# Dilated attention's entry reordered, and the stick attention's scores split over both halves of the array's rows

## The chip, the cores and the metric

One core of a Trainium2 chip runs the whole program. The engines work beside each other and meet through semaphores: TensorE (PE; its weight loads are the rows PEld) multiplies into the eight banks of PSUM, VectorE (DVE), ScalarE (ACT) and GpSimd (POOL) do the elementwise work, and SyncE (SP) issues the weight loads. The metric is device microseconds of one execution, the median of the runs. TensorE's clock is granted at one of two levels, 1.2 or 2.4 GHz; the profile gives the granted share.

## What is computed

Two blocks of two layers each on 512 tokens of width 1024: a state-space mixer and a stick-breaking attention with their gated MLPs, then an even mixer (a chunked gated MLP beside a dilated attention) and a gated linear attention with convolutional MLPs. The change touches the stick attention and the entry of the even mixer's dilated attention:

```python
# stick-breaking attention, 16 heads of 64; per block of 128 queries
z = jnp.einsum('bhqd,bhkd->bhqk', qb, kb) * scale
log_beta = jax.nn.log_sigmoid(z)
log_1m_beta = jnp.where(past, jax.nn.log_sigmoid(-z), 0.0)
between = lax.cumsum(log_1m_beta, axis=3, reverse=True) - log_1m_beta
weights = jnp.where(past, jnp.exp(log_beta + between), 0.0)
outs.append(jnp.einsum('bhqk,bhkd->bhqd', weights.astype(vb.dtype), vb))

# even mixer: gated MLP beside 8 heads of dilated attention
a_out = chunked_gmlp(gelu(u), gelu(v), a_ln_g, a_ln_b, a_ws, a_bs)
qh, kh, vh = rms_norm(heads(q), q_g), rms_norm(heads(k), k_g), heads(vb)
# three branches of softmax(qk / 8) v with windows and strides, mixed by their log-sums
out = jnp.concatenate([a_out, b_out], axis=-1).astype(h.dtype) @ w_out
```

## The kernel before

Each engine has its own program, written out stage by stage, and waits by hand on counting semaphores; nothing is scheduled by a tool. Weights come as tiles of 1 MB, two buffers in turn. Each is split into a rounded high part (ScalarE, L1562) and the rest (VectorE, L2207), and a product of two such numbers is three matmuls (hi x hi, hi x lo, lo x hi). Plain 32-bit operands take two passes over the array for one matmul, so the trace shows twice as many matmuls as the program has.

**Stick attention** (`stick_attention`, L1104 to L1170). Q and K lie with the features on partitions, two heads of 64 features one above the other: an even head on rows 0 to 63, an odd one on rows 64 to 127. `stick_scores(h)` writes the scores of head h, keys on partitions, into the three banks 4 (h mod 2) to 4 (h mod 2) + 2: a mask matmul (L1109), then the four blocks of a key block with its own queries (L1114, first bank), then the later queries of key blocks 0, 2 and 1 (L1120, 384, 128 and 256 columns; second and third bank). All have 64 rows, those of the head. The loop runs scores of head h+1, the running sums of head h (`stick_sums`, L1130 to L1142), then half a mix of an earlier pair of heads (`stick_mix`, L1153 or L1161) from h = 2 on. VectorE and ScalarE work on each head's scores in two parts, own blocks and later queries: absolute value (L2389), exponential (L1680), logarithm (L1686), combination (L2398), and after the sums the weights' exponential (L1693). `z_done` counts the scores' two releases, `w_done` the two halves of weights, after which the banks are free. Before, the mask waits for the first half of head h-2's weights and the later queries for the second. GpSimd is idle in this stretch.

**Entry of dilated attention.** After the q and k features of the even mixer (stage ev_qk) TensorE does the gated MLP's products (L1210, `gm_bank` 5, 6, 7, 3) and eight mean squares of the heads' q and k (L1220, banks 0 to 3 in turn). VectorE adds the bias (L2569) and multiplies into `u_feat` (L2573, `gm_copied`); then it builds the table of score biases (L2575 to L2588). ScalarE squares the features (L1778), takes the logarithms of the mean squares (L1780, `qk_ln`) and one exponential over all (L1783, `qk_rstd`); VectorE then scales q and k of two pairs of heads (`stage_pair`, L2618). TensorE waits for all eight logarithms, computes the values (stage ev_vb, `token_stage`: eight units of 24 matmuls on 128 tokens and 256 columns, banks 0 to 7, L1088 to L1090), and only then the scores of heads 0 and 1 (L1234). VectorE adds the biases and takes the row maxima (`rows`, L2599, L2603), ScalarE exponentiates (L1790) and normalises (L1797) by VectorE's reciprocal (L2608). Then runs the steady loop of eight heads: transposing the probabilities ("turn", L1244), a copy of them by ScalarE (L1802), scores two heads ahead (L1234), and the product with the values (`mix`, L1255). The weights' splitting for the next stage lies among it: VectorE's second one (L2207) stands between the rows of head 1 and the reciprocal of head 0.

The linear attention of the second block is not touched, but one of its loops is read below: its state products alternate between the two halves of the array's rows, and each half writes its own banks:

```python
for a in range(2):
    for hf in range(2):
        rows = slice(hf * 64, hf * 64 + 64)
        n = 4 * m + 2 * a + hf
        if n < GLA_CHUNKS - 1:
            mm = nc.tensor.matmul(bank[2 * hf + m][:, a * GLA_DV:(a + 1) * GLA_DV], gks_t[rows, n // 2, h, :],
                                  gvt[rows, n // 2, h * GLA_DV:(h + 1) * GLA_DV], start=True, stop=True)
```

## Time and profile before

| | |
|---|---|
| median of 3 runs | 2556.47 us (2555.90 to 2556.67) |
| the profiled execution | 2554.76 us, its span 2553.0 us |
| mean granted clock of TensorE | 0.981 |
| busy share of the span | PE 96%, PEld 79%, DVE 48%, ACT 32%, POOL 12% |
| chain that ended last | PE 89%, DVE 7%, ACT 2%, POOL 1% |

Times in the rows are microseconds from the span's start. A row of the timeline merges equal instructions that follow each other: the first number is the start, the second the length, and x14 says how many. Behind the row stands, in brackets, how long its engine was idle and what ended that.
### The profile page before, as it was taken

The page shows a single profiled execution, that of the slowest core. Times are in us where ns is not written, and L with a number is a line of the kernel's source. Part 1 is how long each engine was busy: PE and PEld are TensorE (multiplying, and loading weights), DVE is VectorE, ACT ScalarE, POOL GpSimd, SP SyncE. Part 2 cuts the span into 40 slices and gives each one's busy share as a digit, 9 for nine tenths or more (in the row PEclk, how much of TensorE's full clock was granted, in tenths as well). Part 3 has the DMA queues.
Part 4 walks back from the last instruction along what each step waited for, and adds up shares of the span by engine and source line. Part 5 has one row for each costly group of instructions (what it writes and reads, how often), then busy time and mean ns, then how long its engine had stood idle before and what let it go on. Part 6 is the DMA issues. An engine that isn't in the chain of part 4 may idle for free.

```text
span 2553.0 us, 32215 instructions
## 1 busy us (share of the span) xinstructions
PE 2459.4 (96%) x12941; PEld 2017.4 (79%) x12941; DVE 1233.3 (48%) x1618; ACT 824.9 (32%) x923; POOL 304.7 (12%) x213
## 2 busy tenths in 40 slices
PE   7699999999999989999989989999999999999999
PEld 6587788887897668888858758888889986988887
DVE  8835433345435564333544464555434445644432
ACT  5422322223225523222243363333323243432222
POOL 6503000004000040000221013000023001100000
PEclk8899999999999989999999989999999999999999
DMA  2432232233320013322342211323233221233232
GB/s 54 92 103 92 83 98 91 77 102 95 99 86 14 11 56 99 99 93 80 91 121 67 67 34 50 108 92 98 85 93 105 83 83 50 83 99 99 84 91 90
DMA packets 254438, 210.30 MB, mean 82 GB/s; under 512 B 7156, under 2 KB 252298, under 8 KB 254250
## 3 DMA queue, kind: packets, MB, share of 16 engines
q1 hardware_dynamic: 250682, 205.99, 26.2%
q8 instruction: 102, 1.67, 0.3%
q0 software_dynamic: 976, 1.74, 0.3%
q10 hardware_dynamic: 2656, 0.72, 0.1%
q14 instruction: 22, 0.18, 0.0%
HBM read 203.97 MB, written 2.10 MB: 81 GB/s over the span
## 4 chain that ended last, share of the span: by engine, by line
PE 89%; DVE 7%; ACT 2%; POOL 1%; issue 1%; DMA 0%; SPq 0%; DVEq 0%; POOLq 0%; ACTq 0%
PE psum L845 14%; PE psum L847 14%; PE psum L846 14%; PE psum L975 9%; PE psum L976 9%; PE psum L977 9%; PE psum L1088 2%; PE psum L1089 2%; PE psum L1090 2%; POOL tmp_a L575 1%; PE psum L1120 1%; PE psum L1138 1%; PE psum L926 1%; PE psum L927 1%; PE psum L928 1%
## 5 line engine op out<-in xcount | busy, mean ns | idle before, releaser
L1562 ACT CAST w_hi<-w_stage 128x2048 fp32r<-128x2048 f32 x209 | 400.4, 1916 | 1341.2 <-PE psum L847 714.5
L2207 DVE TENSOR_TENSOR w_lo<-w_stage,w_hi 128x2048 fp32r<-128x2048 f32 x202 | 473.8, 2345 | 634.5 <-ACT w_hi L1562 634.4
L975 PE MATMUL psum<-x_hi,w_hi 128*128 128x512 f32 x864 | 341.1, 395 | 19.9 <-DVE x_lo L2343 16.1
L845 PE MATMUL psum<-x_hi,w_hi 128*128 128x512 f32 x888 | 345.9, 390 | 0.0
L846 PE MATMUL psum<-x_lo,w_hi 128*128 128x512 f32 x888 | 345.5, 389 | 0.0
L847 PE MATMUL psum<-x_hi,w_lo 128*128 128x512 f32 x888 | 345.5, 389 | 0.0
L976 PE MATMUL psum<-x_lo,w_hi 128*128 128x512 f32 x864 | 339.7, 393 | 0.0
L977 PE MATMUL psum<-x_hi,w_lo 128*128 128x512 f32 x864 | 339.3, 393 | 0.0
L845 PE MATMUL psum<-hidden_hi,w_hi 128*128 128x512 f32 x746 | 291.4, 391 | 0.8 <-DVE w_lo L2207 0.8
L847 PE MATMUL psum<-hidden_hi,w_lo 128*128 128x512 f32 x746 | 290.3, 389 | 0.0
L846 PE MATMUL psum<-hidden_lo,w_hi 128*128 128x512 f32 x746 | 290.2, 389 | 0.0
L975 PEld LDWEIGHTS psum<-x_hi,w_hi 128*128 128x128 f32 x864 | 164.4, 190 | 58.4 <-issue 23.5
L845 PEld LDWEIGHTS psum<-x_hi,w_hi 128*128 128x128 f32 x888 | 166.7, 188 | 35.2 <-issue 0.7
L847 PEld LDWEIGHTS psum<-x_hi,w_lo 128*128 128x128 f32 x888 | 166.7, 188 | 34.7
L846 PEld LDWEIGHTS psum<-x_lo,w_hi 128*128 128x128 f32 x888 | 166.7, 188 | 34.4
L977 PEld LDWEIGHTS psum<-x_hi,w_lo 128*128 128x128 f32 x864 | 164.3, 190 | 34.7
L976 PEld LDWEIGHTS psum<-x_lo,w_hi 128*128 128x128 f32 x864 | 164.5, 190 | 34.0
L845 PEld LDWEIGHTS psum<-hidden_hi,w_hi 128*128 128x128 f32 x746 | 140.0, 188 | 30.8 <-issue 2.1
L846 PEld LDWEIGHTS psum<-hidden_lo,w_hi 128*128 128x128 f32 x746 | 140.0, 188 | 29.5 <-issue 0.5
L847 PEld LDWEIGHTS psum<-hidden_hi,w_lo 128*128 128x128 f32 x746 | 140.0, 188 | 29.2
L565 POOL TENSOR_TENSOR tmp_a<-residual 128x512 f32<-128x512 f32 x4 | 7.2, 1793 | 945.3 <-DVE residual L2252 831.0
L1088 PE MATMUL psum<-w_hi,x_hi 128*128 128x256 f32 x384 | 109.6, 285 | 0.8 <-ACT qk_rstd L1780 0.8
(436 smaller groups left out, 3437.9 us busy)
## 6 DMA issues: line engine op xcount, KB each, us to landing
w_stage<-in_ffn_w_gu_dram SPq DMA_DIRECT2D x44, 1024.0 KB, 5.1
w_stage<-in_ffn_w_down_dram SPq DMA_DIRECT2D x64, 704.0 KB, 4.6
w_stage<-in_ffn_w_gate_dram SPq DMA_DIRECT2D x22, 1024.0 KB, 5.2
w_stage<-in_ffn_w_up_dram SPq DMA_DIRECT2D x22, 1024.0 KB, 5.4
w_stage<-in_sb_w_qkv_dram SPq DMA_DIRECT2D x12, 1024.0 KB, 5.1
w_stage<-in_od_w_in_dram SPq DMA_DIRECT2D x12, 1024.0 KB, 5.3
w_stage<-in_ev_w_in_dram SPq DMA_DIRECT2D x10, 1024.0 KB, 5.1
w_stage<-in_ssm_w_glu_dram SPq DMA_DIRECT2D x8, 1024.0 KB, 5.5
```

Source lines behind the costliest of these rows:

```text
L575: sum_link(nc.gpsimd.tensor_tensor(acc_sq, acc_sq, dev_slot[c], ALU.add))
L845: nc.tensor.matmul(dst, hi, x_hi, start=(start and k == 0), stop=False)
L846: nc.tensor.matmul(dst, hi, x_lo, start=False, stop=False)
L847: mm = nc.tensor.matmul(dst, lo, x_hi, start=False, stop=(stop and k == kn - 1))
L975: nc.tensor.matmul(dst[u], hi, x_hi, start=(k == order[0]), stop=False)
L976: nc.tensor.matmul(dst[u], hi, x_lo, start=False, stop=False)
L977: mm = nc.tensor.matmul(dst[u], lo, x_hi, start=False, stop=(k == order[-1]))
L1088: nc.tensor.matmul(dst, hi, wh[:, k, :], start=(k == 0), stop=False)
L1089: nc.tensor.matmul(dst, hi, wl[:, k, :], start=False, stop=False)
L1090: mm = nc.tensor.matmul(dst, lo, wh[:, k, :], start=False, stop=(k == DC - 1))
L1562: nc.scalar.copy(whi[:, half, :], wst[:, half, :]).then_inc(whi_done, 1)
L2207: V.tensor_tensor(wlo[:, half, :], wst[:, half, :], whi[:, half, :].bitcast(F32), ALU.subtract).then_inc(wlo_done, 1)
```

## The change

**Scores on both halves of the rows.** Two new tiles of 2 KB a partition, `q_swapped` and `k_swapped`, hold one head's q and k on the half of the partitions that is not its own. GpSimd fills them by two DMAs a head (64 partitions of 2 KB, SBUF to SBUF): heads 0 and 1 once the k stage is done, head h from the end of head h-2's scores, each pair after the pair before has landed (`swap_landed`). `stick_scores` now waits, before the first own block, for both halves of head h-2's weights and for the copies. Then it runs own block 0, the later queries of key block 0 on the other half, own blocks 1 and 2, the later queries of key block 2 on the other half, own block 3 (first release) and the later queries of key block 1 on the own half (second release).

**Entry of dilated attention.** The mean squares go to banks 0, 1, 2 and 4, and chunk 3 waits for the first product of the gate instead of the fourth. The values' banks are 5, 6, 7, 3 for the first half of the columns and 4, 0, 1, 2 for the second; the first half waits for the gate's banks one by one, only the second half for all logarithms. The scores of heads 0 and 1 stand behind the first and second unit of the second half and use the first half's banks. VectorE's rows, reciprocals and value copies are woven into that order, both of its splits of the next stage's weights come later, and ScalarE normalises head 0 before it exponentiates head 1; ScalarE's two casts of the weight tiles stand before head 0 and after head 1.

```diff
-                half = slice((h % 2) * 64, (h % 2) * 64 + 64)
+                own, other = slice(h % 2 * 64, h % 2 * 64 + 64), slice(64 - h % 2 * 64, 128 - h % 2 * 64)
...
                 if h >= 2:
                     pe.wait_ge(w_done, 2 * (h - 2) + 2)
...
+                pe.wait_ge(swap_landed, 32 * (h + 1))
+                own_block(0)
+                later_queries(0, other, k_swap, q_swap)
+                own_block(1)
+                own_block(2)
+                later_queries(2, other, k_swap, q_swap)
+                own_block(3).then_inc(z_done, 1)
+                later_queries(1, own, k_f[:, h // 2, :], q_f[:, h // 2, :]).then_inc(z_done, 1)
```

```diff
+            pool.wait_ge(evac_done, ST["k"].evac1)
+            for h in range(HEADS):
+                own, other = slice(h % 2 * 64, h % 2 * 64 + 64), slice(64 - h % 2 * 64, 128 - h % 2 * 64)
+                if h >= 2:
+                    pool.wait_ge(z_done, 2 * (h - 2) + 2)
+                if h >= 1:
+                    pool.wait_ge(swap_landed, 32 * h)
+                pool.dma_start(q_swap[other, :], q_f[own, h // 2, :]).then_inc(swap_landed, 16)
+                pool.dma_start(k_swap[other, :], k_f[own, h // 2, :]).then_inc(swap_landed, 16)
```

```diff
                     if c == 3:
 
-                        pe.wait_ge(gm_copied, 4)
+                        pe.wait_ge(gm_copied, 1)
...
+                pe.wait_ge(wlo_done, st.it0 * 2 + 1)
+                for n in range(TT):
+                    pe.wait_ge(gm_copied, n + 1)
+                    value_unit(0, n)
+                pe.wait_ge(wlo_done, st.it0 * 2 + 2)
+                pe.wait_ge(qk_ln, 8)
+                for n in range(TT):
+                    value_unit(1, n)
+                    if n < 2:
+                        early_scores(n)
```

How the order changes, at the places that are spoken of below. On TensorE, one steady round of the stick attention before, from the mask to the first sum:

```order
L1109 MATMUL psum<-not_past,ident_rounded 128x512 [waits w_done]
L1114 MATMUL psum<-q_feat,k_feat 128x128 x4
L1120 MATMUL psum<-q_feat,k_feat 128x384 [waits w_done]
L1120 MATMUL psum<-q_feat,k_feat 128x128
L1120 MATMUL psum<-q_feat,k_feat 128x256
```

The same round now (q_swapped and k_swapped are the other half of the rows):

```order
L1125 MATMUL psum<-not_past,ident_rounded 128x512 [waits w_done]
L1131 MATMUL psum<-q_feat,k_feat 128x128 [waits swap_landed,w_done]
L1135 MATMUL psum<-q_swapped,k_swapped 128x384
L1131 MATMUL psum<-q_feat,k_feat 128x128 x2
L1135 MATMUL psum<-q_swapped,k_swapped 128x128
L1131 MATMUL psum<-q_feat,k_feat 128x128
L1135 MATMUL psum<-q_feat,k_feat 128x256
```

The second wait for the weights moved from the later queries to the first own block, and the two matmuls of the other half stand among the own blocks.

On VectorE, from the last scaled pair of heads to the first reciprocal, before (prob is a head's rows, value_tok the values):

```order
L2618 SCALAR_TENSOR_TENSOR kn_pair<-qk_feat,params,qk_rstd 128x512
L2219 UNCONDITIONAL_BRANCH
L2378 COPY value_tok<-psum 128x256 [waits part_done] x4
L2207 TENSOR_TENSOR w_lo<-w_stage,w_hi 128x2048 [waits whi_done]
L2378 COPY value_tok<-psum 128x256 [waits part_done] x4
...
L2603 TENSOR_REDUCE even_stats<-prob 128x1 [waits sm_done]
L2207 TENSOR_TENSOR w_lo<-w_stage,w_hi 128x2048 [waits whi_done]
L2608 RECIPROCAL even_stats<-even_stats 128x4 [waits pexp]
```

The same place now; the rows left out at the two dots are those of heads 0 and 1:

```order
L2649 COPY value_tok<-psum 128x256 [waits part_done] x4
...
L2649 COPY value_tok<-psum 128x256 [waits part_done]
L2665 RECIPROCAL even_stats<-even_stats 128x4 [waits pexp]
...
L2649 COPY value_tok<-psum 128x256 [waits part_done]
L2261 TENSOR_TENSOR w_lo<-w_stage,w_hi 128x2048 [waits whi_done]
L2649 COPY value_tok<-psum 128x256 [waits part_done] x2
L2261 TENSOR_TENSOR w_lo<-w_stage,w_hi 128x2048 [waits whi_done]
L2705 UNCONDITIONAL_BRANCH
L2665 RECIPROCAL even_stats<-even_stats 128x4 [waits pexp]
```

The first reciprocal moved ahead of both splits, and the second one, of head 1, stands behind both.

## Rows read from the trace of the kernel before

**Rows 1.** Stage table, stick attention: stretch, length, busy time by engine (count), clock, DMA, GB/s

```profile
788.80:886.20 97.40, 97.40 (x573) 64.55 (x572) 58.00 (x101) 55.85 (x79) 0.00 (x0) 1.00 0.00 1
```

**Rows 2.** Timeline, one head's scores, and the weights that free the next banks

```profile
801.89 1.16 PE L1114 MATMUL psum<-q_feat,k_feat 64*128 64x128 f32 x8
...
802.88 1.46 PE L1120 MATMUL psum<-q_feat,k_feat 64*128 64x384 f32 x6
...
804.28 1.12 PE L1130 MATMUL psum<-stick,neg_up_to 128*128 128x512 f32 x2
...
808.05 0.81 ACT L1693 ACTIVATE stick<-psum 128x768 f32<-128x768 f32 x1 [0.52 <-PE psum L1142]
...
809.41 1.16 PE L1114 MATMUL psum<-q_feat,k_feat 64*128 64x128 f32 x8
```

**Rows 3.** Timeline of TensorE, state products of the linear attention, two heads

```profile
2084.99 0.49 PE L1350 MATMUL psum<-gla_v_tok,gla_k_tok 64*128 64x256 f32 x2
...
2092.62 1.99 PE L1350 MATMUL psum<-gla_v_tok,gla_k_tok 64*128 64x256 f32 x14
```

**Rows 4.** Timeline, the same round, VectorE's first and ScalarE's last step on the scores

```profile
803.08 0.69 DVE L2389 TENSOR_SCALAR stick<-psum 128x512 int32<-128x512 int32 x1
...
806.60 0.93 ACT L1686 ACTIVATE stick<-stick,one_col 128x768 f32<-128x768 f32 x1
```

**Rows 5.** Timeline, a round without a mix

```profile
780.02 0.81 ACT L1693 ACTIVATE stick<-psum 128x768 f32<-128x768 f32 x1 [0.52 <-PE psum L1142]
...
780.15 1.16 PE L1114 MATMUL psum<-q_feat,k_feat 64*128 64x128 f32 x8
...
786.43 1.16 PE L1114 MATMUL psum<-q_feat,k_feat 64*128 64x128 f32 x8
```

**Rows 6.** Line L603: two 128 KB loads on GpSimd's queue, issue ns and landing us

```profile
L603 POOL DMA_DIRECT2D d_rows<-in_ev_a_bs_dram x2: 627/640/654, 1324.8 to 1325.5; - x2
...
DMA to landing us min/median/max: 4.4/4.4/4.4
```

**Rows 7.** Timeline of TensorE at the entry of dilated attention

```profile
1443.37 1.19 PE L1220 MATMUL psum<-even_squares,head_mean 128*128 128x512 f32 x1 [3.77 <-DVE u_feat L2573]
...
1451.62 0.38 PE L1088 MATMUL psum<-w_hi,x_hi 128*128 128x256 f32 x1 [0.78 <-ACT qk_rstd L1780]
...
1486.39 2.57 PE L1244 MATMUL psum<-ident,prob 128*128 128x128 f32 x10 [6.09 <-ACT prob L1797]
...
1497.54 1.31 PE L1244 MATMUL psum<-ident,prob 128*128 128x128 f32 x10
...
1503.43 0.77 PE L1244 MATMUL psum<-ident,prob 128*128 128x128 f32 x5
```

**Rows 8.** Timelines of VectorE and ScalarE at the entry of dilated attention

```profile
1438.55 0.69 DVE L2573 TENSOR_TENSOR u_feat<-u_feat,mixed 128x512 f32<-128x512 f32 x1
...
1440.63 0.69 ACT L1780 ACTIVATE qk_rstd<-psum,eps_rms 128x512 f32<-128x512 f32 x1
...
1475.00 1.91 ACT L1562 CAST w_hi<-w_stage 128x2048 fp32r<-128x2048 f32 x1 [9.61 <-PE psum L1090]
...
1476.08 0.29 DVE L2599 SCALAR_TENSOR_TENSOR prob<-psum,score_bias 128x128 f32<-128x128 f32 x1 [0.70 <-PE psum L1234]
...
1479.16 0.69 DVE L2603 TENSOR_REDUCE even_stats<-prob 128x1 f32<-128x512 f32 x1
...
1483.44 2.28 DVE L2207 TENSOR_TENSOR w_lo<-w_stage,w_hi 128x2048 fp32r<-128x2048 f32 x1
...
1485.84 1.93 ACT L1797 ACTIVATE prob<-prob,even_stats 128x128 f32<-128x128 f32 x4 [1.47 <-DVE even_stats L2608]
```

**Rows 9.** Stage table, entry of dilated attention: the same columns as rows 1

```profile
1443.40:1450.80 7.40, 7.40 (x10) 2.84 (x10) 4.06 (x11) 3.27 (x5) 0.00 (x0) 0.60 0.01 2
1451.60:1474.90 23.30, 23.28 (x192) 23.08 (x192) 7.73 (x12) 5.54 (x2) 0.00 (x0) 1.00 0.14 46
...
1486.40:1497.50 11.10, 11.10 (x26) 5.49 (x26) 4.09 (x9) 6.83 (x16) 0.00 (x0) 0.52 0.29 94
```

More of the change, by code:

```diff
@@ L2370, in copy_stage, with token_stage @@
                 stage_loop(name, body)
[L2372 removed]
+            def token_stage(name, dst):
                 st = ST[name]
@@ L2379, in body @@
                                           bank[4 * half + n][:, 0:256]).then_inc(evac_done, 1)
-                        if not (hold and half):
-                            split_next(half)
+                        split_next(half)
                 stage_loop(name, body)
@@ L2636, in dilated_attention @@
                 stage_pair(0, 1)
-                values()
-                rows(0, 0)
-                rows(1, 1)
-                split(ST["ev_vb"].it0 + 1, 1)
+                for n in range(TT):
+                    value(0, n)
+                rows(0, 0, first_scores)
+                value(1, 0)
                 sums(0, 0)
+                rows(1, 1, first_scores)
+                value(1, 1)
+                split(st.it0 + 1, 0)
+                value(1, 2)
+                value(1, 3)
+                split(st.it0 + 1, 1)
                 with dve.Fori(0, HEADS_B // 4 - 1) as i:
```

84 lines of the change are left out of this document (53 added, 31 removed).

## The prediction

> **What bounds the kernel now.** I read the page's chain first, then the two stretches that the diff touches. The chain is nearly all TensorE: work taken from TensorE, or a stall taken from it, moves the end. The stick attention is such work: from 788.8 to 886.2 TensorE is busy all the time at the full clock while VectorE and ScalarE are busy 58.0 and 55.9 of 97.4 us [rows 1]. The entry of dilated attention is the other kind. There TensorE stands idle 3.77 us for `u_feat`, then runs at a fallen clock, then waits 6.09 us for the first head's `prob`, and again runs at half clock [rows 7, 9]. A reader should see in both that what ends late is named in the row: TensorE itself in the first, ScalarE and VectorE in the second.
>
> **Stick scores.** One head's scores are eight passes for the own blocks from 801.89 to 802.88 (0.99 us) and six for the later queries until 804.28, where the sums start; 0.09 of that is the turn to a full-height load, so 1.30 [rows 2]. Those six passes stream 1536 columns, 0.85 ns a column: 0.11 us for 128 columns, 0.22 for 256, 0.32 for 384, with 0.11 for the first weight load. All use one half of the array's rows. The change puts the later queries of key blocks 0 and 2 (two passes of 0.32, two of 0.11) on the other half. If the halves run beside each other, the own half is the longer one: 0.11 + 8 x 0.11 + 2 x 0.22 = 1.43 us instead of 2.29 (0.86 with rounding). Do they? The state products of the second block's linear attention alternate between the halves at 64 rows and 256 columns: the first two passes, 0.48 us each, lie within 0.49 us; and fourteen passes take 1.99 us, where in a row they would take 0.11 + 14 x 0.22 and a tail of 0.16, 3.35 us, and where the half with eight passes alone gives 0.11 + 8 x 0.22 + 0.16 = 2.03 [rows 3]. So the longer half sets the time, and I take 0.86 for each of 16 heads, 13.8 us; with no overlap it is nothing, which stays as the other bound.
>
> The Trainium skill ("TensorE: Matmul & The Clock Gate", Packing small matmuls) says that matmuls start and end strictly in program order, one FIFO for all tiles. By that rule the third to sixth own passes wait behind the long pass of the other half and a head's scores take about 1.65 us. The rows speak against it: in program order the second pass of the lower half stands ahead of the first of the upper half, yet the first passes of both lie in 0.49 us.
>
> What it adds: the own blocks now also wait for the second half of the weights of head h-2 (w_done, from L1693). At the steady pace ScalarE ends that one at 808.86 and the own blocks start at 809.41 [rows 2]: 0.55 us to spare. Queued behind the waiting matmul are all of TensorE's sums. Cover is gone where there is no mix yet: there L1693 runs from 780.02 to 780.83 and the own blocks started at 780.15 [rows 5]. The scores' first release comes no earlier than before (own block 3 ends with the eighth pass of its half in both), so the loop through VectorE and ScalarE must be walked too: own blocks to L2389 1.19, on to the second L1686 3.52, that one 0.93, L1693 0.81, and about 0.1 to TensorE: 6.55 us a head [rows 2, 4]. TensorE's period there is 809.41 less 801.89 = 7.52, after the change 6.66: still the longer, by 0.1. In the rounds without a mix it is 6.28 [rows 5], would be 5.4, and the loop wins: counted in old times, head 2's own blocks start at 780.3 (L1693 is ready 0.6 earlier, since the sums are), head 3's 6.55 later at 786.9 instead of 786.43, and its scores end at 788.3 instead of 788.7. Heads 1 to 3 together gain 0.4 instead of 2.6. So 0.86 (head 0, among value matmuls) + 0.4 + 12 x 0.86 = **11.6 us**.
>
> The copies: 32 of 128 KB on GpSimd's queue, none in the trace. The nearest row is a 128 KB load on that queue, 0.64 us to issue and 4.4 to land [rows 6]; two in flight, about 5.5 us. The copy for head h goes out when the scores of h-2 are done and is wanted nearly two periods (some 12 us) later; GpSimd has nothing else there until the next norm, and the DMA engines move 1 GB/s [rows 1]. I take them at zero; what they cost if late is a rival.
>
> **Entry of dilated attention.** Step one: the mean square of chunk 3 waits for the first of L2573 (ends 1439.24) instead of the fourth; it started at 1443.37, and the next ten passes ran at a mean clock of 0.60 [rows 7 to 9]. Freed, its two passes of 512 columns (0.43 each) end at about 1440.4, and the rest is paced by ScalarE: busy with the logarithm of chunk 2 until 1441.32, then one square and five logarithms of up to 0.69, started a little closer [rows 8], to about 1444.8. The last mean square is out by 1443.8; the values take other banks and start at about 1443.9 instead of 1451.62: 7.7 us.
>
> Step two: the 192 value passes stay 23.1 us [rows 9], and two heads' scores go between them, 2.4 us each (twice 1280 columns at 0.85 ns, and 0.2 for the load and the turn). Rows, exponentials and normalising of head 0 run beside the value units of 2.9 us. So the values end at 1443.9 + 23.1 + 4.8 = 1471.8, with the turns back to the values' form 1472.2, and turn 0 follows at 1472.3 instead of 1486.39: 14.1 us.
>
> Step three: turn 0 to turn 1 took 11.15 us, of which nearly all at a clock of 0.52; at the full clock a round takes 1497.54 to 1503.43, 5.9 [rows 7, 9]. With no idle stretch ahead I expect the full clock, 6.05 with the waits: 5.1 more, **19.2 us** at turn 1. Head 1's `prob` is the narrow point: ScalarE casts the second weight tile (1.91) only after 1472.3, VectorE splits it (2.28) until 1476.6, then ScalarE normalises (1.93) until 1478.8 [rows 8]. Turn 1's last transposes wait for that.
>
> Step four, given back: head 2's rows (3.8 us, as head 0's from 1476.08 to 1479.85) [rows 8] start only at 1476.8, so its exponentials end about 1481.6, ahead of which ScalarE may not copy turn 1: 1.0 us; and stage_pair ends behind head 3's rows, 0.8 us late for head 4's scores. After that TensorE is the longest again. 19.2 - 1.8 = **17.4 us**. Bounds: 19.2 if VectorE keeps up, 9.3 if the clock falls as before (below).
>
> Sum: 17.4 + 11.6 = 29.0. The profiled execution took 2554.8 us (span 2553.0); it would take 2525.8. The median of the runs is 1.7 above it, so 2556.5 - 29.0 = **2527.5 us**.
>
> **Rivals.**
> - Starts in order. A pass of the upper half does not overtake waiting passes of the lower. Then, from the first load, own 0 starts at 0.11 and 0.22, the long passes at 0.22 and 0.54, own 1 and 2 from 0.54 to 0.88, the other half's short ones at 0.88 and 0.99, own 3 at 0.99 and 1.10, the last two at 1.21 and 1.43, and the end is 1.65 instead of 1.43: 0.2 less saved on 13 heads, 2.8 us: 2530. For it: one pair of passes and one total are thin evidence. Against: [rows 3]. The skill's FIFO rule, above, is this case.
> - No overlap at all: the scores cost 2.29 as before. 2539. Against: [rows 3]; for: there each product wrote its own bank from fresh, here they add to a bank with a mask.
> - The loop through VectorE and ScalarE binds. 6.55 against 6.66 is close, and every second head VectorE evacuates a mix ahead of L2389. If every round costs half a microsecond more, the attention gains 5: 2534.
> - The clock falls again at the entry, since ScalarE paces the mean squares and head 1's `prob` is late. Then the two cold stretches stay, 3.0 us of the first (7.4 x 0.4) and 5.1 of the second: 2535.6.
> - **Slower than before:** the copies. Head h's go out only when those of h-1 have landed, so a round can't be shorter than one pair's issue and landing. If two 128 KB copies don't overlap, 2 x (0.64 + 4.4) = 10.1 us a round [rows 6] against 7.7 before (the 97.4 us of [rows 1] hold twelve such rounds and a short one of 4.7): 14 x 2.4 = 33 us. With the scores' gain gone and the entry's 17.4 left the kernel takes 2572. From a pair time of 7.7 + 17.4 / 14 = 8.9 us it is slower than before; below 6.6 the copies cost nothing. Against: loads on this queue were in flight together when their 4.4 was taken.
>
> **How the numbers follow.** Forecast 0.66 (its own range 2522 to 2533), starts in order 0.10, no overlap 0.05, the loop 0.09, the clock 0.07, slower 0.03. The fastest end is the full 13.8 and 19.2, 2523.5, less 2 us for clock changes elsewhere, since all later idle stretches shift: 2521. The upper end, 2537, takes in all rivals but no overlap and the copies. A measurement of this kernel tells 0.2% (5 us) from no change. Only the copies reach that bound or cross it: faster 0.96, same 0.01, slower 0.03.
>
> **What would show it.** In the stick attention: 1.5 us from the first own pass to the sums, 0.86 us less between the sums of successive heads, no wait of TensorE longer than 0.2 us except in the first two rounds, copies landing in 3 to 6 us. At the entry: the value matmuls start 7 to 8 us earlier after the gate's, there is no idle over 1.5 us, the clock is 1.0 throughout, and turn 1 comes 34 us after the first value matmul instead of 45.9. Wrong if the passes of the two halves follow each other, if TensorE waits for `swap_landed`, if the gap before turn 1 is over 2 us, or if the stage after the entry gives the time back waiting for weights.

## The result, and the profile after

The changed kernel takes 2524.45 us (median of 4 runs, 2523.96 to 2528.27) against 2556.18 (2553.92 to 2556.67) for the kernel before beside it. The ratio is 0.9881, 95% interval 0.9864 to 0.9898. The profiled execution took 2524.61 us, 30.15 less than the profiled one of before. The forecast was 2527.5.

The page of the changed kernel, its span and the granted clock in 40 slices:

```profile
span 2522.9 us, 32268 instructions
...
PEclk9899899999999999999999999999999999999999
```

To see where 30.1 us went, I took four marks from the timelines of both kernels: the first mask of the stick attention, the end of its last running sums (L1138, now L1162), the gate's first matmul (L1210, now L1234), the end of the last mix of dilated attention. The offset is the time after less the time before.

| mark | before | after | offset | gained since the mark above |
|---|---|---|---|---|
| first mask | 762.08 | 765.18 | +3.10 | -3.1 |
| last sums end | 889.32 | 879.95 | -9.37 | **12.46** |
| gate's first matmul | 1432.28 | 1420.51 | -11.77 | 2.4 |
| last mix ends | 1537.17 | 1507.03 | -30.14 | **18.37** |
| end of the span | 2553.0 | 2522.9 | -30.1 | 0 |

The two bold stretches are what the diff touches. The other two entries belong to code that is the same in both kernels. There the granted clock differs: from 240 to 260 us it is 1.00 before and 0.83 after; from 946 to 962 it is 0.74 before, and in the same work of after, 938 to 950, 0.86; from 1332 to 1348 it is 0.89 before, and in the same work of after, 1323 to 1339, 1.00. They nearly cancel.

The two changed stretches, busy times of each engine, then the granted clock. First before:

```profile
762.08:889.32 127.24, 127.24 (x752) 87.70 (x751) 75.11 (x130) 70.29 (x96) 0.00 (x0) 1.00 0.03 9
...
1432.28:1537.17 104.89, 90.53 (x482) 60.08 (x481) 61.15 (x121) 63.19 (x125) 10.22 (x12) 0.90 0.09 31
```

and after:

```profile
765.18:879.95 114.77, 113.43 (x752) 78.12 (x751) 73.91 (x130) 67.54 (x96) 14.41 (x28) 1.00 0.17 42
...
1420.51:1507.03 86.52, 82.39 (x482) 57.31 (x481) 60.51 (x120) 62.26 (x125) 10.19 (x12) 1.00 0.11 37
```

In the first, TensorE's instructions are the same in number (752) and its busy time fell by 13.8 us; 1.34 us of idle time is new. In the second, the clock rose from 0.90 to 1.00 and TensorE's idle time fell from 14.4 to 4.1 us.

**One head's scores** in the changed kernel, TensorE's timeline (the counterpart of [rows 2]; L1131 are the own blocks, L1135 the later queries, L1154 the sums):

```profile
795.05 0.37 PE L1131 MATMUL psum<-q_feat,k_feat 64*128 64x128 f32 x1
...
795.06 0.59 PE L1135 MATMUL psum<-q_swapped,k_swapped 64*128 64x384 f32 x1
...
795.26 0.38 PE L1131 MATMUL psum<-q_feat,k_feat 64*128 64x128 f32 x2
...
795.48 0.48 PE L1135 MATMUL psum<-q_swapped,k_swapped 64*128 64x384 f32 x1
...
795.49 0.49 PE L1131 MATMUL psum<-q_feat,k_feat 64*128 64x128 f32 x3
795.80 0.27 PE L1135 MATMUL psum<-q_swapped,k_swapped 64*128 64x128 f32 x1
...
796.04 0.59 PE L1135 MATMUL psum<-q_feat,k_feat 64*128 64x256 f32 x2
...
796.57 1.12 PE L1154 MATMUL psum<-stick,neg_up_to 128*128 128x512 f32 x2
```

Both halves start within 0.01 us. From the first own pass to the sums it is 1.52 us, where before it was 2.39. In the program the second long pass of the swapped tiles stands ahead of the second own block; in the trace it waits for its half until 795.48, while the own pass behind it began at about 795.37 (the second of the two at 795.26, 0.11 apart). So a waiting pass of one half doesn't stop the other half. The Trainium skill ("TensorE: Matmul & The Clock Gate", Packing small matmuls) says that matmuls keep program order in start and in end; this timeline disagrees on the start, and the measurement decides. (The ends of matmuls are modelled in the trace, so it says less of them.)

**The entry**, TensorE's timeline from the mean squares to the scores of head 4 (the counterpart of [rows 7]; L1244 mean squares, L1269 the early scores, L1302 turns, L1313 mixes, L1292 later scores):

```profile
1424.98 7.16 PE L1244 MATMUL psum<-even_squares,head_mean 128*128 128x512 f32 x16
...
1446.45 2.42 PE L1269 MATMUL psum<-kn_pair,qn_pair 64*128 64x128 f32 x8
...
1460.09 1.25 PE L1302 MATMUL psum<-ident,prob 128*128 128x128 f32 x10
...
1465.92 1.39 PE L1302 MATMUL psum<-ident,prob 128*128 128x128 f32 x10
...
1470.32 2.37 PE L1313 MATMUL psum<-prob_t,vb_pair 128*64 128x512 f32 x8 [0.65 <-ACT prob_t L1854]
1472.61 1.31 PE L1302 MATMUL psum<-ident,prob 128*128 128x128 f32 x10
1474.67 2.39 PE L1292 MATMUL psum<-kn_pair,qn_pair 64*128 64x128 f32 x8 [0.74 <-issue]
```

All sixteen mean squares run in one piece and the values follow at 1431.58. Turn 0 starts 39.57 us after the gate's first matmul (before: 54.11), turn 1 at 45.41 (before: 65.25). The last two rows with brackets are the only new waits.

### The profile page after: what moved, and what is told of

It is laid out like the page before. It is cut to its first block, busy times and chain, and to the rows that moved or that the text cites. A ratio compares the mean times of both kernels' runs of the same rounds, so it can differ in the third digit from the quotient of the medians.

```text
span 2522.9 us, 32268 instructions
## 1 busy us (share of the span) xinstructions
PE 2439.9 (97%) x12941; PEld 2005.0 (79%) x12941; DVE 1231.4 (49%) x1617; ACT 820.6 (33%) x923; POOL 321.0 (13%) x245
## 4 chain that ended last, share of the span: by engine, by line
PE 90%; DVE 4%; ACT 2%; POOL 2%; issue 1%; SPq 1%; DMA 0%; POOLq 0%; DVEq 0%; ACTq 0%
PE psum L861 15%; PE psum L862 15%; PE psum L863 15%; PE psum L991 9%; PE psum L992 9%; PE psum L993 9%; PE psum L1104 2%; PE psum L1105 2%; PE psum L1106 2%; POOL tmp_a L581 1%; SPq L451 1%; PE psum L942 1%; PE psum L1162 1%; PE psum L943 1%; PE psum L944 1%
## 5 line engine op out<-in xcount | busy, mean ns | idle before, releaser
L2261 DVE TENSOR_TENSOR w_lo<-w_stage,w_hi 128x2048 fp32r<-128x2048 f32 x202 | 473.8, 2345 | 631.2 <-ACT w_hi L1614 631.2
L861 PEld LDWEIGHTS psum<-hidden_hi,w_hi 128*128 128x128 f32 x746 | 140.0, 188 | 31.1 <-issue 2.1
L2292 DVE TENSOR_TENSOR tmp_b<-psum,tmp_a 128x512 f32<-128x512 f32 x52 | 36.0, 692 | 120.8 <-PE psum L863 120.8
```

Source lines behind the costliest of these rows:

```text
L861: nc.tensor.matmul(dst, hi, x_hi, start=(start and k == 0), stop=False)
L2261: V.tensor_tensor(wlo[:, half, :], wst[:, half, :], whi[:, half, :].bitcast(F32), ALU.subtract).then_inc(wlo_done, 1)
L2292: V.tensor_tensor(tmp_b[:, u, :], bank[2 + u][:, :], tmp_a[:, u, :], ALU.mult).then_inc(evac_done, 1)
```

## The experiments

The runs were taken in three groups, each beside its own runs of the kernel before, whose medians were 2555.6 (e1 to e4), 2556.58 (e5 to e8) and 2555.03 us (e9 to e12). The medians scatter by 2 us or so with the clock elsewhere, so beside each median stands the length of the two stretches of the table, which repeat to 0.02 us.

| run | median us | ratio, 95% interval | stick attention | dilated attention |
|---|---|---|---|---|
| before | 2556.18 | | 127.24 | 104.89 |
| changed | 2524.45 | 0.9881 (0.9864 to 0.9898) | 114.78 | 86.52 |
| e1_scores_only | 2540.58 | 0.994 (0.9924 to 0.9957) | 114.78 | 103.11 |
| e2_entry_only | 2539.18 | 0.9935 (0.9919 to 0.9952) | 127.24 | 86.52 |
| e3_copies_own_half | 2536.86 | 0.9923 (0.9906 to 0.9939) | 130.39 | 86.53 |
| e4_bunched | 2524.85 | 0.988 (0.9864 to 0.9897) | 116.34 | 86.53 |
| e5_split_late | 2528.82 | 0.9889 (0.9866 to 0.9912) | 114.78 | 87.44 |
| e6_mean_square_wait | 2531.15 | 0.9905 (0.9888 to 0.9924) | 114.78 | 93.11 |
| e7_scores_behind_values | 2531.72 | 0.9906 (0.9888 to 0.9923) | 114.78 | 95.57 |
| e8_own_first_heads_2_3 | 2525.43 | 0.9882 (0.9864 to 0.9901) | 113.87 | 86.53 |
| e9_changed_again | 2523.21 | 0.9881 (0.9865 to 0.9898) | 114.78 | 86.53 |
| e10_improved | 2520.14 | 0.9869 (0.9852 to 0.9885) | 113.85 | 85.09 |
| e11_copies_late | 2523.96 (one run) | | 114.78 | 86.53 |
| e12_other_half_last | 2527.78 (one run) | | 119.88 | 86.53 |

### The two parts alone

e1 is the kernel before with the swapped tiles, their copies and the new score order; e2 is the changed kernel with the old scores.

> The kernel before with the stick attention's part of the change alone: the two swapped tiles, their 32 copies on GpSimd, and the seven score calls in the new order over both halves of the rows. The entry of dilated attention is the old one (its semaphore `tables` is folded into sm_done, at the same place). My theory, that the two parts add and that the whole trace difference of 30.1 us is 12.5 in the stick attention (from the first mask to the last sums 124.2 against 111.7 us), 18.4 at the entry, and the rest clock changes of 3 us of either sign elsewhere: 2556.2 - 12.5 = 2543.7, within 3 us; sums 6.65 and 7.06 us apart, as in the changed kernel. The prediction's own term was 11.6: 2544.6. Rival 1, the attention's gain comes only together with the new entry (its part is given back before the entry, at a wait for weights): 2553 or more. Rival 2, most of the 30 us is the attention and the entry alone brings under 12: 2538 or less.

> The changed kernel with the old stick scores: no swapped tiles, no copies, fourteen passes on one half of the rows. The entry of dilated attention is the new one. My theory: 18.4 us less than before, 2537.8, within 3 us; the prediction's term was 17.4, 2538.8. Turn 1 comes 45.4 us after the gate's first matmul as in the changed kernel, and TensorE's clock is 1.0 there. Rival, the clock's good behaviour at the entry is luck of the phase, and depends on when the stage begins: with the stage 12 us later one cold stretch of 6.8 us returns, 3.4 us lost, 2541.2 or more.

Measured: 15.0 and 16.4 us less than before, 31.4 together, against 31.1 for the changed kernel by the same runs of before. In the stretches the parts add exactly: 12.46 in the stick attention with or without the new entry, 18.37 at the new entry with or without the new scores. The old entry in e1:

```profile
1417.50:1520.60 103.10, 88.74 (x482) 59.38 (x481) 61.12 (x120) 63.03 (x125) 10.22 (x12) 0.92 0.10 31
```

It takes 103.1 us instead of 104.9, with the clock at 0.92 instead of 0.90: the old entry's cost depends on how its idle stretches fall on the clock. The new entry in e2, which begins 11.8 us later than in the changed kernel, keeps the full clock:

```profile
1432.30:1518.80 86.50, 82.37 (x482) 57.28 (x481) 60.51 (x120) 62.24 (x125) 10.18 (x12) 1.00 0.11 37
```

All eight profiles that have the new entry without further changes keep 1.00 through it, with the gate's first matmul at 1416.7 to 1434.4 us. So the rival that its good clock was luck of the phase is not borne out; how near it is, e6 shows below.

### Is it the two halves, or something that came with them?

```diff
-                own_block(0)
-                later_queries(0, other, k_swap, q_swap)
-                own_block(1)
-                own_block(2)
-                later_queries(2, other, k_swap, q_swap)
-                own_block(3).then_inc(z_done, 1)
+                own_block(0)
+                own_block(1)
+                own_block(2)
+                own_block(3).then_inc(z_done, 1)
+                later_queries(0, own, k_f[:, h // 2, :], q_f[:, h // 2, :])
+                later_queries(2, own, k_f[:, h // 2, :], q_f[:, h // 2, :])
```

> The changed kernel, copies and waits kept, but the later queries of key blocks 0 and 2 read the original tiles on the own half of the rows, and all own blocks come first, as before. Nothing overlaps, so the difference to the changed kernel is the worth of the two halves, and the difference to the run with the new entry alone is what the copies and the two waits ahead of the own blocks cost. My theory: copies 0; the earlier wait for the second half of the weights makes the rounds of heads 2 and 3 take the loop's 6.55 us instead of 6.28, 0.5 us in all: 0.5 us above the entry alone, so about 2538.3 and 13.8 (0.86 times 16) above the changed kernel. Rival, the copies cost (TensorE waits for swap_landed, or their traffic slows the weights' loads): 3 us or more above the entry alone.

The stick attention took 130.39 us, 3.15 more than before and 15.6 more than the changed kernel. TensorE never waits for the copies. Of the 3.15 us, the rounds of heads 2 and 3 account for 1.48: sums 7.03 us apart instead of 6.29. The other 1.7 go with a fall of the clock between 788 and 796 us (0.79 over 8 us). It shows in the sums 2.4 us behind the second of two waits of 0.67 us. The changed kernel has the same two waits, the same copies and no such fall, so the cause stays open. The rival on the copies had named 3 us or more, which is the size; but no wait for a copy is in the trace. The median lies below e2's in spite of it; with the clock elsewhere differing, the medians can't tell 3 us here.

My price for the earlier wait was wrong: 0.74 us a round, not 0.27. The timeline of e3 in the round of head 2, ScalarE and TensorE:

```profile
779.85 0.81 ACT L1745 ACTIVATE stick<-psum 128x768 f32<-128x768 f32 x1 [0.52 <-PE psum L1166]
...
780.72 1.16 PE L1131 MATMUL psum<-q_feat,k_feat 64*128 64x128 f32 x8 [0.67 <-ACT stick L1745]
```

The second exponential of the weights, L1745, is released by TensorE's own last sums (L1166), not by the logarithm. The loop that binds is scores (2.38), sums until that exponential may start (3.77), the exponential (0.81) and the step back to TensorE (0.06): 7.02. In the changed kernel it is the same chain with 1.52 for the scores, 6.16:

```profile
777.60 1.12 PE L1154 MATMUL psum<-stick,neg_up_to 128*128 128x512 f32 x2
...
781.38 0.81 ACT L1745 ACTIVATE stick<-psum 128x768 f32<-128x768 f32 x1
...
782.24 0.37 PE L1131 MATMUL psum<-q_feat,k_feat 64*128 64x128 f32 x1 [0.67 <-ACT stick L1745]
```

### The loop of the first rounds

If it is that chain, own blocks that don't wait for L1745 shorten it. They write only the first bank, which the first half of the weights frees.

```diff
+                if h in (2, 3):
+                    own_block(0)
+                    own_block(1)
+                    own_block(2)
+                    own_block(3).then_inc(z_done, 1)
                 if h >= 2:
                     pe.wait_ge(w_done, 2 * (h - 2) + 2)
                 pe.wait_ge(swap_landed, 32 * (h + 1))
+                if h in (2, 3):
+                    later_queries(0, other, k_swap, q_swap)
+                    later_queries(2, other, k_swap, q_swap)
+                    later_queries(1, own, k_f[:, h // 2, :], q_f[:, h // 2, :]).then_inc(z_done, 1)
+                    return
```

> The changed kernel, but for heads 2 and 3 (the rounds that have no mix) the four own blocks come first and only then the wait for the second half of the weights and for the copies; the later queries follow as in the bunched run. It tests what binds those rounds. In the changed kernel the sums of heads 2 and 3 come 6.16 us after the previous ones: 1.52 of scores, 3.78 of sums until ScalarE may start its second exponential of weights (0.81), and the own blocks wait for that. My theory: it is this chain, so with the own blocks ahead of the wait the rounds take 5.6 us each, 1.1 us less in all, 2523.4. The prediction's theory, the way through |z|, exponential and logarithm on VectorE and ScalarE binds at 6.1 to 6.5: the rounds stay at 6.1 or more, 2524.5.

The rounds take 5.70 and 5.72 us, 0.91 less together. The timeline of e8, where L1755 is the exponential of the weights and L1164 the sums:

```profile
779.56 0.81 ACT L1755 ACTIVATE stick<-psum 128x768 f32<-128x768 f32 x1
...
779.68 0.93 PE L1131 MATMUL psum<-q_feat,k_feat 64*128 64x128 f32 x6
780.42 0.59 PE L1135 MATMUL psum<-q_swapped,k_swapped 64*128 64x384 f32 x1
...
781.49 1.12 PE L1164 MATMUL psum<-stick,neg_up_to 128*128 128x512 f32 x2
```

The own blocks start while L1755 runs, and only the later queries wait for its end at 780.37. VectorE and ScalarE keep up at 5.7 us a round, so the prediction's 6.55 for the way through them was no bound.

### How far a pass runs ahead

Two runs move the calls of the other half towards the end of the list.

e4:

```diff
-                later_queries(0, other, k_swap, q_swap)
                 own_block(1)
                 own_block(2)
-                later_queries(2, other, k_swap, q_swap)
                 own_block(3).then_inc(z_done, 1)
+                later_queries(0, other, k_swap, q_swap)
+                later_queries(2, other, k_swap, q_swap)
                 later_queries(1, own, k_f[:, h // 2, :], q_f[:, h // 2, :]).then_inc(z_done, 1)
```

e12 puts the last of these three lines ahead of the other two, so that ten passes of the own half come first.

> The changed kernel with the same seven score calls in another order: four own blocks first (with the first release), then the later queries of key blocks 0 and 2 on the other half, then those of block 1 on the own half. It tells how far a pass can run ahead of waiting passes of the other half. In the changed kernel the two halves' calls alternate in the program. A, each half has a line of its own of any length: 1.52 us from the first own pass to the sums as in the changed kernel, and its time, 2524.5. B, passes are handed out in program order and only one or two wait at each half (my theory, since the second pass on the other half stood waiting while own passes ran on): the other half gets its first pass when the own blocks are nearly through, at about 0.8 to 1.0 us, needs 0.86 us, and the last call of the own half runs beside it; 1.9 to 2.0 us, that is 0.4 to 0.5 more on 13 heads, 2530. C, no overlap at all once bunched: 2.39 us, 0.86 more on 13 heads and more, 2536.

> The changed kernel with all calls of the own half first (four own blocks, then the later queries of key block 1: ten passes), and both calls of the other half last. It measures how far a pass can run ahead in the program's order. In the bunched run the first pass of the other half began 0.55 us after the first own pass, when five of the eight own passes ahead of it had begun. A, a fixed number of passes (about three) may wait in front of it: it begins when the last own block's second pass begins, at about 0.88 us, needs 0.86 us, and the sums start 1.8 to 1.9 us after the first own pass. B, it is handed out as soon as its weights can be loaded, whatever waits: 0.55 us again, and 1.6 us to the sums. C, long passes ahead close the window: no overlap, 2.39 us.

One head in e4:

```profile
801.90 0.82 PE L1131 MATMUL psum<-q_feat,k_feat 64*128 64x128 f32 x5
802.45 0.59 PE L1135 MATMUL psum<-q_swapped,k_swapped 64*128 64x384 f32 x1
...
802.89 0.59 PE L1135 MATMUL psum<-q_feat,k_feat 64*128 64x256 f32 x2
803.20 0.38 PE L1135 MATMUL psum<-q_swapped,k_swapped 64*128 64x128 f32 x2
803.51 1.12 PE L1154 MATMUL psum<-stick,neg_up_to 128*128 128x512 f32 x2
```

and in e12:

```profile
795.32 1.04 PE L1131 MATMUL psum<-q_feat,k_feat 64*128 64x128 f32 x7
796.10 0.59 PE L1135 MATMUL psum<-q_swapped,k_swapped 64*128 64x384 f32 x1
...
797.16 1.13 PE L1154 MATMUL psum<-stick,neg_up_to 128*128 128x512 f32 x2
```

In e4 the other half's first pass begins 0.55 us in, when the fifth of eight own passes has begun; in e12 0.78 us in, when the seventh of ten has. Both times three passes of the own half stand in front of it, waiting. So in both orders a pass overtakes three and no more; that three is the limit in general rests on these two orders alone. From the first own pass to the sums: 1.61 and 1.84 us, against 1.52 in the changed order and 2.39 in one half. My B for e4 gave 1.9 to 2.0: the reach is longer than I took it. Case A of e12 held in its number of passes and in the 1.84 us; the start came 0.10 us earlier than it said.

The order has a second consequence. In e4 the second release hangs on the last call of the list (own half, 802.89 to 803.48), but the other half's last pass, which stands ahead of it in the program, ends only at 803.58. VectorE began to read these banks at 803.70. In the changed order the other half is through first, at 796.18 against 796.63. With passes that overtake, a release on the last call says nothing of the other half by itself: look in the timeline which half ends last. Whether the release waits for both, no run here shows.

### The copies

```diff
-                if h >= 2:
-                    pool.wait_ge(z_done, 2 * (h - 2) + 2)
                 if h >= 1:
+                    pool.wait_ge(z_done, 2 * (h - 1) + 2)
                     pool.wait_ge(swap_landed, 32 * h)
```

> The changed kernel with the copies for head h sent when the scores of head h-1 are done, not those of h-2. It measures how much cover the copies need, for the rival that they hold the loop up. From the release (about 1.5 us after the first own pass) to the issue 0.4, two issues of 0.52 and 2.2 to 2.4 us to land: the second copy has landed about 4.8 us after the first own pass, against rounds of 6.16 to 7.06. My theory: the sums stay 6.16, 6.65 and 7.06 us apart and nothing waits; stick attention 114.8 us. Rival, a pair costs what the prediction's slow case took, 8.9 us and more: rounds of over 8 us.

Nothing waits; all rounds are those of the changed kernel to 0.01 us. In the changed kernel the copies of q, from issue to landing:

```profile
DMA to landing us min/median/max: 2.1/2.2/5.7
```

Those of k have a median of 2.4, at most 6.5. A pair is there some 3 us after its issue. The slow rival's turning point, 8.9 us, is far off.

### The entry, step by step

e6 restores one wait:

```diff
-                        pe.wait_ge(gm_copied, 1)
+                        pe.wait_ge(gm_copied, 4)
```

> The changed kernel with the one wait restored: the mean square of chunk 3 waits again for all four u_feat instead of the first. Banks and all else stay new. It measures step one. My theory: mean square 3 starts 11.1 us after the gate's first matmul as before, the clock falls for what follows, and the values start 16.7 to 18.0 after the gate's instead of 11.07 (the run with the new scores alone had 18.1 there, with the wait for the last logarithms on top); the loss stays to the end: 5.6 to 7, so 2530 to 2531.5, and the end of the last mix at 92.1 to 93.5. Rival, TensorE catches up, since the head loop was waiting for VectorE and ScalarE anyway: 3 us or less lost, 2527.5. Rival 2, the fallen clock persists into the value matmuls: more than 8 us lost, 2532.5 or more.

```profile
1431.59 6.23 PE L1244 MATMUL psum<-even_squares,head_mean 128*128 128x512 f32 x10 [3.77 <-DVE u_feat L2626]
...
1431.60:1437.30 5.70, 5.70 (x11) 2.44 (x11) 4.05 (x10) 2.88 (x5) 0.00 (x0) 0.70 0.01 3
```

The same 3.77 us of waiting as in the kernel before is back, and the clock of the mean squares behind it falls to 0.70. The values start 16.75 us after the gate's first matmul instead of 11.07, and the last mix ends 6.59 later. The 5.68 us at the values' start stay to the end. The other 0.9 come 39 us after the values' start, at head 1's mix:

```profile
1476.00 4.06 PE L1313 MATMUL psum<-prob_t,vb_pair 128*64 128x512 f32 x8 [0.65 <-ACT prob_t L1854]
```

```profile
1476.00:1479.50 3.50, 3.50 (x6) 1.24 (x7) 3.43 (x7) 3.50 (x11) 0.00 (x0) 0.52 0.01 3
```

The clock falls there, and eight passes take 4.06 us instead of 2.37; in exchange the wait of 0.74 us behind it is gone. In the changed kernel and seven other runs the same wait of 0.65 us left the clock at 1.00. So the one restored wait is worth 5.7 of the 18.4 us, and 6.6 if the second fall is its doing, which isn't shown. The other 2.6 us at the values' start (16.75 here, 19.34 in the kernel before) are the wait for the last logarithm, which the new banks take away, and a clock of 0.60 instead of 0.70 [rows 9].

e7 keeps step one and undoes the interleaving:

```diff
                 for n in range(TT):
                     value_unit(1, n)
-                    if n < 2:
-                        early_scores(n)
+                early_scores(0)
+                early_scores(1)
```

> The changed kernel with the two early scores behind all eight value units instead of between them. It measures the interleaving, steps two and three. Walk: values end 34.3 us after the gate's first matmul; head 0's scores, rows (3.8), exponentials and normalising follow, so turn 0 begins at about 40.0 instead of 39.57; head 1's rows end at 43, both splits of VectorE (4.6) stand ahead of its reciprocal, normalised at 50, so turn 1 ends some 3.3 later than now. My theory: 3.5 to 4.5 us slower than the changed kernel at the full clock, 2528.5, end of the last mix at 90 to 91. Rival, the clock falls in the new gaps (it did in the kernel before, with a gap of 6.1 us there): 7 or more slower, 2531.5 or more. Rival 2, the order doesn't matter, since the scores need no time of their own: within 1 us of the changed kernel.

The last mix ends 9.05 us later, the median is 7.3 above the changed kernel's: the first rival. TensorE's row of turn 0, and the window of that round:

```profile
1464.48 2.37 PE L1302 MATMUL psum<-ident,prob 128*128 128x128 f32 x10 [3.88 <-DVE prob L2656]
```

```profile
1464.40:1478.00 13.60, 12.26 (x34) 6.80 (x35) 9.72 (x16) 8.17 (x18) 3.16 (x2) 0.53 0.49 155
```

A wait of 3.88 us, and the whole round after it runs at 0.53: turn 0 to turn 1 takes 12.65 us instead of 5.84. By an estimate about 5.8 of the 9.05 us are the clock (12.26 busy at 0.53). The rest, 3.3, is idle time: turn 0 starts 3.6 us later, the round holds about 1 us of waits more, and the changed kernel's two waits behind it (1.4 us) are gone. That is the pattern of the kernel before, with 6.09 us of wait and 0.52 [rows 7, 9]. More than half of what e7 loses is the clock.

### What is given back, and a faster version

Why do the two waits at 1470.32 and 1474.67 remain? VectorE in the changed kernel (L2261 the split, L2665 the reciprocal of the sums, L2675 stage_pair):

```profile
1462.27 2.29 DVE L2261 TENSOR_TENSOR w_lo<-w_stage,w_hi 128x2048 fp32r<-128x2048 f32 x1 [1.56 <-ACT w_hi L1614]
1464.48 0.17 DVE L2665 RECIPROCAL even_stats<-even_stats 128x4 f32<-128x4 f32 x1
...
1473.83 0.74 DVE L2675 SCALAR_TENSOR_TENSOR kn_pair<-qk_feat,params,qk_rstd 128x512 f32<-128x512 f32 x1
```

and ScalarE (L1849 the normalising of head 1, L1854 the copy of turn 1):

```profile
1464.69 1.92 ACT L1849 ACTIVATE prob<-prob,even_stats 128x128 f32<-128x128 f32 x4 [1.32 <-DVE even_stats L2665]
...
1469.06 1.20 ACT L1854 COPY prob_t<-psum 128x1280 f32<-128x1280 f32 x1
```

Head 1's exponentials were done at 1457.02, yet its reciprocal stands behind a split of weights that nobody needs for 40 us. e5 moves that split:

```diff
                 def heads4(i, first, last):
                     for hd in range(4):
+                        if last and hd == 2:
+                            split(st.it0 + 1, 1)
...
                 value(1, 3)
-                split(st.it0 + 1, 1)
```

> The changed kernel with one line moved: VectorE's second split of the coming weights stands before the last two heads' work instead of ahead of the head loop. It tests the prediction's step four, that this split (2.3 us) and what queues behind it give back part of the entry's gain. My theory: the reciprocal of head 1, head 2's rows and stage_pair run earlier, and TensorE's two remaining waits of the entry, 0.65 us ahead of head 1's mix and 0.74 us ahead of head 4's scores, both vanish: from the gate's first matmul to the end of the last mix 85.1 us instead of 86.5, and 2523.1. Rival, what is given back is ScalarE's doing (its cast of 1.91 us stands ahead of the copy of turn 0): the first wait stays, 0.7 less only. Rival 2, the weights' buffer comes free some 30 us later and the next stage waits for its second load: 1 to 5 us more after the attention, 2525 or more.

Both waits vanish: turn 3 comes 57.36 us after the gate's first matmul instead of 58.78, 1.42 less, as expected. But the last mix ends at 87.44, not at 85.1. The split now stands ahead of the evacuation of the last pair but one:

```profile
1498.05 2.28 DVE L2261 TENSOR_TENSOR w_lo<-w_stage,w_hi 128x2048 fp32r<-128x2048 f32 x1
...
1500.34 0.66 DVE L2594 CAST x_hi<-psum 128x512 fp32r<-128x512 f32 x1
```

and TensorE waits 2.06 us for that evacuation, after which its clock is 0.66 for 5 us. None of my three theories had it. The median, 2528.8 with runs from 2523.95 to 2532.1, also holds a slower clock elsewhere in the program.

e10 puts the split one head later, behind that evacuation (`if last and hd == 3`), where VectorE has nothing to do for 7.8 us, and takes the order of e8 for heads 2 and 3. e9 is the changed kernel beside it.

> The changed kernel itself, as the measure for the run beside it, on the same chip. Its stick attention should take the same 114.8 us from the first mask to the last sums and its dilated attention the same 86.5 us, to 0.05 us. My theory: what differs between executions of one program here is TensorE's clock in the stretches outside the two changed ones: the profiled span minus half the sum of its half-clock stretches should be the same as in the first profile within 1.5 us. Rival: DMA arrival differs, and the two stretches themselves vary by 0.3 us or more. Time 2524 to 2529.

> The changed kernel with two improvements that the runs point to. Heads 2 and 3 of the stick attention have their own blocks ahead of the wait for the second half of the weights (0.91 us less in the stick attention, as in the run of that alone), and VectorE's second split of the coming weights stands behind the evacuation of the next to last pair, where VectorE has 7.8 us with nothing to do, instead of ahead of the head loop (1.42 us less up to turn 3, as in the run with the late split; that run lost 2.1 us in turn because its split stood ahead of that evacuation, which this one doesn't). My theory: 113.9 us from the first mask to the last sums, 85.1 us from the gate's first matmul to the end of the last mix, 2.3 us less than the changed kernel in these stretches; in the median, where the clock elsewhere makes 2 us either way, between the same and 4.5 us less. Rival, the next stage then waits for its second weight load: more than 0.5 us of wait of TensorE in the 20 us after the last mix.

```profile
761.73:875.59 113.86, 113.86 (x752) 78.86 (x751) 73.75 (x130) 67.39 (x96) 14.38 (x28) 1.00 0.17 42
1418.66:1503.75 85.09, 82.25 (x482) 57.32 (x481) 60.78 (x120) 62.08 (x125) 10.23 (x12) 1.00 0.12 38
```

2520.14 us (2518.26 to 2522.17) against 2523.21 (2522.05 to 2527.3) for the changed kernel: 3.1 less in the median, 2.4 of which are the two stretches. The ratios to before, 0.9869 and 0.9881, have intervals that overlap; that it is faster rests on the stretches, which repeat to 0.02 us. In the stick attention TensorE is now busy all the time, and no wait for the weights' load follows the last mix.

My theory on e9 held for the stretches. For the rest it said that the span less half of the half-clock time should be equal. With the half-clock time that the two traces record, 60.2 us in the first profile and 77.8 in this one, it differs by 10 us, at spans that differ by 1. But the first trace's record of the clock begins only at 37.8 us, and a window ahead of it reads as full clock:

```profile
15.00:38.00 23.00, 14.82 (x128) 14.15 (x125) 21.52 (x62) 11.79 (x24) 12.58 (x10) 1.00 0.13 24
```

In e9 the same window says 0.63, with half clock from 19.2 to 36.3 us. The first trace's own matmuls show where its clock rose:

```profile
37.06 0.63 PE L745 MATMUL psum<-ident,bl_cross 128*128 128x128 f32 x2
...
37.88 0.39 PE L745 MATMUL psum<-ident,bl_cross 128*128 128x128 f32 x2
```

With e9's 17.1 us put in, an estimate, the first profile has 77.3, and the two differ by 1.3 us, inside the 1.5 that I had allowed. So nothing here speaks against the sum of low-clock time as a measure, once the record is whole; check the pace of equal matmuls before you trust a 1.00 at a trace's start.

## Why the prediction was right

**The own half sets the time.** Predicted 1.43 us and 0.09 for the turn to a full-height load, 1.52 together; measured 1.52. The scores of 14 of the 16 heads take 0.87 us less of TensorE's time, as forecast (0.86). e3, with everything but the other half, loses it all.

**The first rounds.** This is the term that was mis-sized. Predicted 0.4 us for heads 1 to 3, measured 1.13 (0.87 + 0.13 + 0.13), since the rounds of heads 2 and 3 take 6.16 us and not 6.55. The step that failed is the walk of the loop: it ran through the logarithm, whose start I took from the old distance to the first L2389. The second |z| starts earlier when the scores end earlier, and what releases L1693 is TensorE's own sums, as its row in [rows 5] already said (0.52 of idle time, ended by L1142). With that chain (3.78 us from the first sums, at 776.24 in the trace of before, to L1693 at 780.02) the sum would have been 1.52 + 3.78 + 0.81 + 0.05 = 6.16. Attention in all: 12.46 instead of 11.6.

**The copies.** 0, as forecast. They land in 2.2 to 2.4 us, below the 3 to 6 that I had named.

**Entry.** Values start 11.07 us after the gate's first matmul, predicted 11.6: gain 8.3 instead of 7.7, since the mean squares run without a break and were not paced by ScalarE. Turn 0 39.57 after it, predicted 40.0 (14.5 instead of 14.1). The round of turn 0 took 5.84 us, predicted 6.05, at the full clock: turn 1 is 19.84 earlier, predicted 19.2. From the first value matmul to turn 1 it is 34.3 us, predicted 34. Given back: 1.47 us, predicted 1.8, by the two waits and reasons named (0.65 and 0.74 us instead of 1.0 and 0.8); e5 shows it by taking the split away. In all 18.37 instead of 17.4.

Sum of the two: 30.8 instead of 29.0; the clock elsewhere took 0.7 of it back in the profiled pair. Both terms were forecast too small, by 0.9 and 1.0 us, so no error hid another.

**The rivals.** Starts in order: refuted by the timeline of one head, and e4 and e12 show the limit that there is. No overlap: refuted. The loop binds: only in the two rounds without a mix. The clock falls at the entry: not in any profile of the new entry, but e6 and e7 show that it does as soon as one of the two long waits is back. Copies: e11.

The balanced split of the passes, with the last own block on the other half too, wasn't tried: it would let both halves write one bank at once. The Trainium skill ("PSUM — Partial Sum Buffer", PSUM bank collisions raise a hardware error) says that different row tiles may not do that; no run here shows it.

## What to carry to other kernels

When work of half the height bounds TensorE, a copy of the operands in the other half of the partitions can pay if the transfer fits under the loop, as it did here. Write the calls of the two halves alternately (bunching them cost 0.09 us a head, putting one half last 0.32) and let each half write its own bank. Before moving work, follow each wait of the loop to the instruction that releases it in the trace of before, not along the order of the mathematics: a row with its releaser named both the bound that I missed and the cover that I had. At a stage's entry, look first for anything on a shared engine that stands ahead of a short link and is not wanted for long: here one split of 2.3 us, and its new place has to be chosen by what queues behind it too.

## What the runs showed of the hardware

- A pass of one half of the rows overtook three waiting passes of the other half, in both orders tried (e4, e12).
- After a wait of 2.06 us (e5), 3.77 us (e6) and 3.88 us (e7) TensorE's next stretch ran at a clock of 0.66, 0.70 and 0.53; after waits of 0.65, 0.74 and 1.31 us it stayed at 1.00 in the changed kernel. The length of the wait alone doesn't decide: in e6 the clock fell behind a wait of 0.65 us (0.52 from 1476.0 to 1479.5), and in e3 2.4 us behind one of 0.67 (0.79 from 788 to 796).
- Work that is the same in both kernels moved by 3.1 us ahead of the first changed instruction, most of it by the clock between 240 and 280 us (0.91 before, 0.83 after), while the changed stretches repeat to 0.02 us over all runs with the same code and clock. An effect of 1 us is found in a stretch and not in the median of the runs.
- A trace's record of the clock can begin late: the first profile of the changed kernel reads 1.00 up to 37.8 us, but a pair of equal matmuls takes 0.63 us at 37.06 and 0.39 at 37.88.
